# Down products of the experts in 32-column quarters, and 64-wide value products in two column halves

## The reference, cut to what matters

```python
# attention, e.g. the stick-breaking one: 8 heads with values 64 wide
o = jnp.einsum('bhts,bshd->bthd', a.astype(v.dtype), v)      # d = 64
# experts: w1, w3 are 1024 x 512, w2 is 512 x 1024, each 2 MB
for e in range(MOE_EXPERTS):                                 # 16
    hid = jax.nn.silu(x @ w1[e]) * (x @ w3[e])
    y = y + gate[:, e:e + 1] * (hid @ w2[e])
```

## Time and profile before

| | us |
|---|---|
| median of 3 runs (lowest to highest) | 1469.23 (1467.95 to 1471.14) |
| the profiled execution, device time | 1469.25 |
| its span, first to last instruction | 1467.3 |

### The profile page before, as it was taken

The page is one execution under the profiler, slowest core; times in us unless marked ns, Lnnn a source line. Parts: engine busy times, 40 slices in busy tenths (PEclk is TensorE's granted clock), DMA queues, the critical chain, the costliest instruction groups (busy, mean ns, idle before and its releaser), DMA issues.

```text
span 1467.3 us, 27763 instructions
## 1 busy us (share of the span) xinstructions
PE 1286.9 (88%) x11991; PEld 825.1 (56%) x11991; DVE 469.3 (32%) x1130; ACT 290.7 (20%) x703; POOL 165.4 (11%) x216
## 2 busy tenths in 40 slices
PE   6999789959999999948998799989877999999960
PEld 3454345548777777714444444444537777777740
DVE  3057873251000000025346651274542000000007
ACT  2122423210000000012345530242210000000013
POOL 0133100010000000020112221110001000000014
PEclk8997979969999999978999799999877999999995
DMA  9400100069999999772002201030038999999744
GB/s 287 129 10 5 59 1 29 15 230 348 372 371 382 380 379 363 293 240 101 22 15 77 107 15 43 29 119 15 29 102 300 385 375 383 381 381 363 306 136 151
DMA packets 69320, 283.55 MB, mean 193 GB/s; under 512 B 19181, under 2 KB 20253, under 8 KB 61002
## 3 DMA queue, kind: packets, MB, share of 16 engines
q1 hardware_dynamic: 56190, 237.94, 43.9%
q0 software_dynamic: 9216, 31.11, 6.0%
q10 hardware_dynamic: 3788, 12.65, 2.2%
HBM read 257.20 MB, written 24.48 MB: 192 GB/s over the span
## 4 chain that ended last, share of the span: by engine, by line
PE 75%; DVE 11%; issue 6%; DMA 2%; ACT 2%; POOL 2%; POOLq 0%; ACTq 0%; DVEq 0%; SPq 0%
PE bank L1058 24%; PE bank L781 15%; PE bank L1070 14%; PE bank L984 8%; PE bank L931 2%; PE bank L814 2%; PE bank L1043 2%; PE bank L900 2%; DVE slot L1546 1%; POOL slot L1985 1%; DVE h L1846 1%; PE bank L909 1%; DVE stats L1545 1%; PE bank L804 1%; DVE stats L1451 1%
## 5 line engine op out<-in xcount | busy, mean ns | idle before, releaser
L1058 PE MATMUL bank<-arena,slot 128*64 128x96 f32 x8192 | 351.4, 248 | 4.5 <-issue 4.4
L1058 PEld LDWEIGHTS bank<-arena,slot 128*64 128x64 f32 x8192 | 343.6, 138 | 11.0 <-issue 8.2
L781 PE MATMUL bank<-slot,xT 128*128 128x512 f32 x512 | 243.8, 633 | 1.1 <-issue 0.9
L1070 PE MATMUL bank<-slot,arena 128*96 128x512 f32 x512 | 227.4, 597 | 2.4 <-ACT arena L1345 2.4
L781 PEld LDWEIGHTS bank<-slot,xT 128*128 128x128 f32 x512 | 102.3, 205 | 122.9 <-issue 122.3
L1070 PEld LDWEIGHTS bank<-slot,arena 128*96 128x96 f32 x512 | 80.8, 163 | 126.8 <-issue 123.3
L1830 DVE TENSOR_TENSOR arena<-arena,bank 128x384 f32<-128x384 f32 x32 | 17.7, 554 | 353.8 <-ACT arena L1338 353.8
L984 PE MATMUL bank<-slot,normed 128*128 128x512 f32 x256 | 119.1, 620 | 0.2 <-ACT normed L1308 0.2
L1822 DVE TENSOR_TENSOR arena<-bank,params 128x768 f32<-128x768 f32 x32 | 30.6, 958 | 191.2 <-PE bank L1043 191.2
L1338 ACT ACTIVATE arena<-bank 128x384 f32<-128x384 f32 x32 | 15.7, 491 | 366.2 <-PE bank L1058 366.2
L931 PE MATMUL bank<-arena,slot 128*128 128x64 f32 (+5 forms) x520 | 78.4, 284 | 4.6 <-ACT slot L1247 3.7
(11 more groups left out here) (179 smaller groups left out, 1105.4 us busy)
## 6 DMA issues: line engine op xcount, KB each, us to landing
slot<-in_moe_w SPq DMA_DIRECT2D x96, 2048.0 KB, 13.3
expert_rows<-arena ACTq DMA_DIRECT2D x32, 384.0 KB, 8.6
slot<-in_w_in_odd SPq DMA_DIRECT2D x6, 2048.0 KB, 9.9
slot<-in_w_in_even SPq DMA_DIRECT2D x3, 2048.0 KB, 15.9
slot<-in_w_out_even SPq DMA_DIRECT2D x2, 2048.0 KB, 10.2
normed_rows<-slot POOLq DMA_DIRECT2D x8, 512.0 KB, 2.9
out<-arena POOLq DMA_DIRECT2D x16, 256.0 KB, 2.3
slot<-in_w_out_odd SPq DMA_DIRECT2D x2, 2048.0 KB, 7.9
```

Source lines behind the costliest of these rows:

```text
L781: last = nc.tensor.matmul(b[o:o + wide, 0:n], xT[:, k, P * t + o:P * t + o + wide], w[:, k, 0:n], start=(k == 0), stop=(k == KC - 1))
L1058: last = nc.tensor.matmul(bank[o:o + 64, b, CAP * m:CAP * m + CAP], weights(w[par])[:, k, at_:at_ + 64], xgT[:, par, k, :], start=(k == 0) ...
L1070: last = nc.tensor.matmul(bank[0:CAP, 6 + j, :], ghid[:, par, m, :], weights(W2[par], 4)[:, m, 512 * j:512 * j + 512], start=(m == 0), sto ...
```

## The change

Two edits.

1. **Experts' down products by pairs.** The 96 rows of an expert are three thirds of 32 (`QUARTER`). A pair of experts has 2 experts x 3 thirds x 2 halves of the output = 12 pieces of 32 rows x 512 columns; they are put into three waves of four (`WAVES`), each piece in its own 32-column quarter of PE and its own 32 partitions of one bank. A wave is 16 matmuls (32 passes), and the waves use banks 6 and 7 in turn. Wave 0 of a pair needs the first expert alone, wave 1 both, wave 2 the second. PE does wave 0 after `up` of the odd expert, and waves 1 and 2 after `up` of the next even one. ACT copies one bank of 128 x 512 for each wave (four `yrow` buffers in place of two) and stores it in two DMAs (`PIECES`) of 2 KB rows: six for a pair in place of two. The weights w2 go round three buffers, the third in the space of `xT`; SP issues w2 of expert 2 at once, and later two loads of w2 together, after the waves that free them; all loads are written out in place of a loop. The waits of DVE and POOL follow the new counts.
2. **Value products in halves.** At L931, where the values are 64 wide and the tile has 128 rows, each product becomes two with 64 of the probabilities' columns each, in two column halves of PE. The 32-row tile and the 128-wide values stay as they are.

```diff
-W1, W3, W2 = (1, 3), (2, 5), (0, 4)
+W1, W3, W2 = (1, 3), (2, 5), (4, 0)
+QUARTER = CAP // 3
+WAVES = (((0, 0, 0), (0, 1, 0), (0, 2, 0), (0, 0, 1)),
+         ((0, 1, 1), (0, 2, 1), (1, 0, 0), (1, 1, 0)),
+         ((1, 2, 0), (1, 0, 1), (1, 1, 1), (1, 2, 1)))
+PIECES = (((0, 96, 0, 0, 0), (96, 128, 0, 0, 1)), ((0, 64, 0, 32, 1), (64, 128, 1, 0, 0)),
+          ((0, 32, 1, 64, 0), (32, 128, 1, 0, 1)))
+def last_wave(e):
+    return 3 * (e // 2) + 2 + e % 2
...
-        yrow = arena[:, 5888:7936].rearrange("p (r d) -> p r d", r=2)
+        yrow = arena[:, 5888:7936].rearrange("p (r d) -> p r d", r=4)
+        w2_ring = (slot[:, W2[0], :], slot[:, W2[1], :], xT[:, :, :].rearrange("p k n -> p (k n)")[:, 0:4096])
...
+                    w2_ring_load(l, 2)
+                    for e in range(NE):
+                        if e + 2 < NE:
+                            sp.wait_ge(up_done[l], e + 1)
+                            w13_load(l, e + 2, e % 2)
+                        if e >= 2 and e % 2 == 0:
+                            for done in (e - 2, e - 1):
+                                if done + 3 < NE:
+                                    sp.wait_ge(down_done[l], last_wave(done))
+                                    w2_ring_load(l, done + 3)
...
+                    wide = r if w == P else min(r, 64)
                     for i, (vb, kr) in enumerate(blocks):
-                        last = nc.tensor.matmul(out[0:r, w * hd:w * hd + w], probT[0:kr, n % 2, i, 0:r],
+                        for o in range(0, r, wide):
+                            last = nc.tensor.matmul(out[o:o + wide, w * hd:w * hd + w],
+                                                    probT[0:kr, n % 2, i, o:o + wide],
...
-            def down(l, e, par):
...
+            def down(l, p, part):
+                w = 3 * p + part
+                experts_of = (2 * p, 2 * p + 1)[part // 2:1 + (part + 1) // 2]
+                for e in experts_of:
+                    pe.wait_ge(w2_in[l][e % 3], 16 * (e // 3) + 16)
+                pe.wait_ge(ghid_done[l], experts_of[-1] + 1)
+                if w >= 2:
+                    pe.wait_ge(yrow_ready[l], w - 1)
+                for m in range(4):
+                    for c, (q, third, j) in enumerate(WAVES[part]):
+                        w2 = w2_ring[(2 * p + q) % 3].rearrange("p (k n) -> p k n", k=4)
+                        last = nc.tensor.matmul(bank[QUARTER * c:QUARTER * c + QUARTER, 6 + w % 2, :],
+                                                ghid[:, q, m, QUARTER * third:QUARTER * third + QUARTER],
+                                                w2[:, m, 512 * j:512 * j + 512], start=(m == 0), stop=(m == 3))
                 last.then_inc(down_done[l], 1)
...
-                    if e > 0:
-                        down(l, e - 1, (e - 1) % 2)
-                down(l, NE - 1, (NE - 1) % 2)
+                    if e % 2:
+                        down(l, e // 2, 0)
+                    elif e > 0:
+                        down(l, e // 2 - 1, 1)
+                        down(l, e // 2 - 1, 2)
+                down(l, NE // 2 - 1, 1)
+                down(l, NE // 2 - 1, 2)
...
-                nc.scalar.copy(yrow[0:CAP, e % 2, :].rearrange("p (j n) -> p j n", j=2), bank[0:CAP, 6:8, :])\
-                  .then_inc(yrow_ready[l], 1)
-                act.wait_ge(yrow_ready[l], e + 1)
-                act.dma_start(y_dram[l][CAP * e:CAP * e + CAP, :], yrow[0:CAP, e % 2, :])\
-                   .then_inc(y_stored[l][e % 2], 16)
+                nc.scalar.copy(yrow[:, w % 4, :], bank[:, 6 + w % 2, :]).then_inc(yrow_ready[l], 1)
+                act.wait_ge(yrow_ready[l], w + 1)
+                for lo_, hi_, q, row, j in PIECES[part]:
+                    row += CAP * (2 * p + q)
+                    act.dma_start(y_dram[l][row:row + hi_ - lo_, 512 * j:512 * j + 512], yrow[lo_:hi_, w % 4, :])\
+                       .then_inc(y_stored[l][w % 4], 16)
...
-                    dve.wait_ge(down_done[l], e - 1)
+                    dve.wait_ge(down_done[l], last_wave(e - 2))
```

More of the change, by code:

```diff
@@ L426, in stream_kernel @@
         w13_in = [[sem(f"{q}_w13_in{l}") for q in ("even", "odd")] for l in range(2)]
-        w2_in = [[sem(f"{q}_w2_in{l}") for q in ("even", "odd")] for l in range(2)]
+        w2_in = [[sem(f"w2_in{l}{r}") for r in range(3)] for l in range(2)]
         gfin_in = sem("gfin_in")
@@ L474, in stream_kernel @@
         yrow_ready = [sem(f"yrow_ready{l}") for l in range(2)]
-        y_stored = [[sem(f"y_stored{l}{r}") for r in range(2)] for l in range(2)]
+        y_stored = [[sem(f"y_stored{l}{r}") for r in range(4)] for l in range(2)]
         picked_in = [[sem(f"picked_in{l}{t}") for t in range(NT)] for l in range(2)]
@@ L929, in step_A @@
                     out = bank[:, NB + tile % 2, :]
+                    wide = r if w == P else min(r, 64)
                     for i, (vb, kr) in enumerate(blocks):
-                        last = nc.tensor.matmul(out[0:r, w * hd:w * hd + w], probT[0:kr, n % 2, i, 0:r],
-                                                vals[0:kr, vb, c:c + w], start=(i == 0),
-                                                stop=(i == len(blocks) - 1))
+                        for o in range(0, r, wide):
+                            last = nc.tensor.matmul(out[o:o + wide, w * hd:w * hd + w],
+                                                    probT[0:kr, n % 2, i, o:o + wide],
+                                                    vals[0:kr, vb, c:c + w], start=(i == 0),
+                                                    stop=(i == len(blocks) - 1))
                     last.then_inc(out_filled, 1)
@@ L1357, in experts @@
                         own_silu(l, e)
-                        if e > 0:
-                            own_rows(l, e - 1)
-                    own_rows(l, NE - 1)
+                        if e % 2:
+                            own_rows(l, e // 2, 0)
+                        elif e > 0:
+                            own_rows(l, e // 2 - 1, 1)
+                            own_rows(l, e // 2 - 1, 2)
+                    own_rows(l, NE // 2 - 1, 1)
+                    own_rows(l, NE // 2 - 1, 2)
             def step_u():
@@ L2033, in own_tokens @@
                         .then_inc(xg_in[l][e % 3], 16)
-                for r in range(2):
-                    pool.wait_ge(y_stored[l][r], 16 * (NE // 2))
+                for r in range(4):
+                    pool.wait_ge(y_stored[l][r], 32 * (3 * NE // 2 // 4))
                 pool.wait_ge(rows_known, l + 1)
```

30 lines of the change are left out of this document (10 added, 20 removed).

## The result

| | before | after |
|---|---|---|
| median, us | 1469.55 (4 runs) | 1425.81 (4 runs, 1423.47 to 1429.92) |
| profiled execution, us | 1469.25 (span 1467.3) | 1423.47 (span 1421.7) |
| PE, matmuls busy, us | 1286.9 (88%) | 1233.8 (87%) |
| first layer's expert stage, us | 304.5 (331.00 to 635.50) | 281.5 (331.54 to 613.05) |
| between the stages, us | 483.4 | 481.5 |

The ratio is 0.9705 with a 95% interval of 0.9678 to 0.9733. Of the 45.8 us between the profiled executions the two expert stages give 23.0 and 20.8, the attention between them 1.9.

What follows compares the result with a forecast made beforehand. The prediction took PE to pace the expert stages without a wait, with transfers also full. From 1469.25 us: 53.3 gained, less 8, 6 and 1 us, 0 for the value products, makes 38, so 1431 us; 8-in-10 range 1410 to 1455.

Steps and rivals of the forecast that it cites:

- the forecast's own case: Whole kernel: PE's gain less waits for loads and issue idle, 1431 us, taken as 1421 to 1441; chance 0.50.
- The sign that the prediction named for being wrong: Transfers in the expert stages: rate dips not going with changes between w2 and w13 loads; PE's clock falling was the other.
- PE's side of edit 1: Experts' down products: a pair's down work falls from 14.08 to 10.90 us, 50.9 us over 16 pairs, plus 2.4 at stage ends.
- Rival (d): Down waves: four streams beside full transfers run two at a time, 16 pairs 107 us more, 1570 us; chance 0.02.
- The start of the stage: Expert 2's `up`: w2 issued ahead delays w1, PE stalls about 4 us (bounds 0 and 6), -8 us for both layers.
- The steady part: Later experts: transfers need 17.95 us an expert against PE's 17.02; lag beyond slack costs 3 us a layer, -6 us.
- the 9 us of slack: Expert stages: w1 lands 14.4 us after issue and is needed after 23.3 us, so 9 us of lag are free.
- (a): Expert stages: transfers bound at today's rate, 18.61 us an expert whatever the order, PE waits 12 us a layer, 1449 us; chance 0.24.
- (c): Expert stages: smaller 2 KB stores hold up weights, 19.5 us an expert, 1472 us or 1490 us, slower; chance 0.06.
- Issue idle: PE's idle within `up` put down to issue, 4.4 us, may grow with three times as many down passes: -1 us.
- Edit 2: Attention's value products: halves save 14 us of passes, entering and leaving them costs 12 us; 0 us taken.
- rival (b): Expert stages: nothing stalls, extra load hides and dips close, 53 to 54 us gained, 1416 us; chance 0.14.

## Why the prediction was right, point by point

The forecast was 1431 us in a range of 1410 to 1455; 1425.81 came, in the forecast's own case (1421 to 1441). The term of PE was right. The losses set against it were 15 us, 14 of them waits for loads; 8.4 us came (the sum at the end of this section), and under 1 us of them are waits for loads. That the two totals lie near each other, and with them some of the nearness of the time, is luck. The sign that the prediction named for being wrong, dips that do not go with the changes of kind, came as well.

**PE's side of edit 1: right.** Forecast 2 x 11.57 + 10.90 = 34.04 us a pair, measured 34.11. The parts differ a little: the waves take 10.57 and not 10.90, and the turning behind them 1.06 and not 0.86, so what leaving the quarters costs shows up in the next transposes. Sixteen pairs give 16 x 3.11 = 49.8 us where 50.9 were forecast. The wait at the end of a stage went, as forecast: the last 96 passes run without a break,

```profile
602.57 10.48 PE bank L1088 x96
...
618.42 0.97 POOL normed L2068
```

and from PE's end (613.05) to the gather it is now 5.4 us, where it was 4.8; 0 with 1 us either way had been taken. Rival (d), whose 107 us come to 105 by its own terms, is out with the first wave.

**The third buffer: the half that the sum had no line for.** The prediction costed what the extra load at the start does, and not what the buffer is there for. The run with two buffers shows it: some 36 us.

**The start of the stage: forecast 4 us a layer, measured 0.1 to 0.3.** Two reasons. The load came sooner: 18.0 us after its issue, where 20.8 to 22.6 had been worked out from 16.0 plus one more load. And PE came later: in the first layer it lost 1.21 and 1.52 us in issue gaps within the first two `up` and was ready at 364.27, not at 361.5. So the load landed beside a delay. With w2 of expert 2 behind, the second of these gaps is 0.27 us and `up` of expert 2 starts 2.1 and 0.9 us sooner in its stage, but the waits further in take that back.

**The steady part: forecast 3 us a layer, measured 0.1 in the first and none in the second.** The step that failed is the one that tied the dips of the earlier trace rows to the changes of kind, two of them an expert, and kept half of them: 17.95 us for each of some 13 experts. With gathers the need is 17.7 to 17.84 us (the two runs with half of `up`), and after them it is 16.46, below PE's pace of 17.05. The last gather of the first layer goes out at 524.2, some nine experts after the start of the steady part. So the lag grows by 0.65 to 0.79 us an expert, 6 to 7 us in all, and then shrinks; the 9 us of slack that the prediction worked out cover it. The loads agree: w1 lands 14.4 us after its issue for expert 4 and 20.4 us for expert 12. The slack is nearly used up: the w1 of experts 11 and 13 take 24.2 and 23.2 us and land at 523.82 and 558.28, just before and 0.1 us after PE is ready, and 23.3 was the figure from which a PE without gaps would wait. So the frame (pace, need, slack) was right; the need was a little too high, and it was kept for too many experts.

Why the dips went: in the kernel before they lie where one older load is ending and the next have only just gone out. In the run that leaves its loads and their order as they were and takes work from PE, the stretch after the issue of a w1 has 415 GB/s; in the earlier trace rows it has 315. There the loads go out while three older ones are still under way, in the kernel before while one is. The rate of stretches in which neither gathers nor stores were moving, by the number of weight loads that had been issued at least 2.2 us before and had not landed (worked out from the traces' packets in bins of 0.4 us, from the middle of the first layer's stage: 385 to 552.5 before, 383.5 to 558.3 after, 389.55 to 513.35 in the run of before with half of `up`):

```
                          1 load     2 loads    3 loads    4 loads    5 loads
before                    347 GB/s   399        -          -          -
after                     416        416        417        415        -
before, half of up        -          -          421        420        422
```

In the kernel before, 44 of 119 us stood at one load; after, 3 of 74. The number alone does not settle it: the few stretches of after with one load have the full rate, and the kernel before is near it with one load, w2, under way until the next ones go out:

```profile
449.50:452.30 2.80, 2.80 (x56) 2.39 (x52) 0.06 (x1) 0.49 (x1) 0.00 (x0) 1.00 1.02 402
```

What is shown is that the order of the kinds is not the cause, and that the dips go when loads are issued well before the older ones end. What is left of dips after, in that middle part, lies nearly all at the gathers.

**Rivals (a) and (c).** (a) had taken today's rate as a limit; it was PE's demand, as the run of before with a third less traffic (1469.38 us, no gain) and the one with half of `up` (404 GB/s) both show. The Trainium skill, DMA: Bandwidth & Descriptors, section Specifications, gives about 358 GB/s for one core; here 401 to 404 GB/s held over stretches of 35 and 124 us, so the measurement decides. The same page of the Trainium skill, section Bandwidth, which the prediction did not weigh, ties that figure to two cores at once and gives 425 GB/s for 16 MB on one core; the rows here lie nearer to that. (c) asked for 19.4 us an expert; at 17.84 us with gathers and all the smaller stores in place it is out. The store queue went from 3788 to 7884 packets, and its share of the DMA engines' time from 2.2 to 2.5% only.

**Issue idle: forecast 1 us, measured 5.5.** `up`'s idle put down to issue went from 4.4 to 9.9 us. Nine gaps of 0.5 to 1.5 us within `up` carry 9.2 of it, four in the first two `up` of the stages (4.7 us) and five further in (4.5 us); the five go when a third of the traffic goes. The first two gaps of the first layer's stage lie 14 and 23 matmuls ahead of the end of `up`, in this kernel and in the runs with two buffers, with w2 behind and without w3 alike: a place in the program, not a time. That points to instructions that come late to PE (the gaps end 1.3 to 1.6 us after a packet of the instruction queue has landed). Whether full transfers make them late is open: in the kernel before, the idle rose from 4.4 to 5.4 us when a third of the traffic went. No run here changed the instructions' own loading, so all of this stays argued. The Trainium skill, Advanced Engine Details and Errata, section ISA Cache, has instructions come in lines of 16 KB, 256 to a line; the instruction queue's 111 packets of 1.82 MB in all are 16 KB each, and by an estimate from that page's figure PE's 2 x 13335 instructions would be 104 of them.

**Edit 2: forecast 0, measured 0.** The split products kept PE busy for 50.1 us. The page by forms now has:

```profile
L944 PE MATMUL bank<-arena,slot 128*64 128x64 f32 x640 | 36.5, 251 | 3.8 <-ACT slot L1269 3.8
```

That is 13.6 us less, where 14 were forecast (with the 0.101 us that the earlier trace rows give for a pass, in place of 0.105, it would have been 13). Most of it goes to entering the halves. The rows in the attention of the first layer, a head of the fourth tile after and before:

```profile
216.33 0.66 PE L920 MATMUL bank<-const,slot 128*128 128x128 f32 x4
216.91 0.69 PE L944 MATMUL bank<-arena,slot 128*64 128x64 f32 x16
217.53 1.98 PE L998 MATMUL bank<-slot,normed 128*128 128x512 f32 x4
```

```profile
216.31 0.61 PE L909 MATMUL bank<-const,slot 128*128 128x128 f32 x4
216.75 1.00 PE L931 MATMUL bank<-arena,slot 128*128 128x64 f32 x8
217.59 1.94 PE L984 MATMUL bank<-slot,normed 128*128 128x512 f32 x4
```

The halves take 0.62 us to the next line where the eight passes took 0.84, and they start 0.58 us after the transposes before them where it was 0.44. Over the 16 heads of each tile (medians, from the instruction before to the one after) heads of one and two blocks lose 0.10 and 0.08 us, those of three and four gain 0.04 and 0.22: 16 x 0.08 = 1.3 us. The stretch between the stages became 1.9 us shorter and the one ahead of the first 0.5 us longer, which is 1.4 us less together. The sizes of both sides were near: entering cost 0.09 us a head (0.10 forecast), a pair of halves 0.058 us (0.06). The Trainium skill, TensorEngine Tiling (Array Packing), section Key Properties, has a change of mode drain the engine; the 0.09 us agree.

**The sum as it came.** 49.8 for the pairs and 2.4 for the ends make 52.2 us (53.3 forecast); the two expert stages gained 43.8. The 8.4 us between are the 5.5 of issue gaps, under 1 us of waits for loads, and the rest in passes that follow each other a little late, of `up` and in one case of two waves. The forecast had 15 us there. The run without w3 takes the waits for transfers out of the account: 1416 us, which is what rival (b) gave for "nothing stalls", with 5.2 us of issue idle still in it.

## What to carry to other kernels

A transfer rate read while an engine paces the stage can be what that engine asked for, as the 382 GB/s at a DMA share of 0.99 were here; what the transfers can do is measured by taking work from the engine and reading the period that is left. Whether a faster engine will wait is then three numbers: its new pace, the transfers' need, and the slack from issue to use, over as many periods as that need lasts. Read the need for periods of the same traffic: with gathers and without them it differed by 1.4 us an expert. When work is paired, its inputs are held longer: without the buffer that allows that, the pairing kept some 7 of its 44 us here. Look for it before counting the products.

## What was not expected of the hardware

- How far quarters overlapped hung on the order of the passes in the stream: interleaved, four at a time (a wave of 3.5 us); one after the other, two at a time (8.79 us), though 8 passes to a quarter stand in a row.
- The stage is now at the edge of the transfers, which need 17.84 us an expert with gathers and 16.46 without, against PE's 17.05: with PE's need cut from 17.05 to 11.7 us an expert the time fell only from 1425.8 to 1414.0 us.
- In that run PE waits some 9 us in each pair. The granted clock is 0.83 over three whole pairs and 0.50, that is 1.2 GHz, in the 3.33 us after the wait that ends at 414.67; an `up` after such a wait (450.80) takes 7.43 us, where one without a wait takes 5.43 (from 462.79 to 468.22); in the changed kernel, with no such waits, the rows have 1.00.
